# Routed experts: one bf16 one-hot picks bias, position and router weight rows from tables in three parts, the selection is finished on VectorE, and the down projection runs in one piece

## The reference, cut to what matters

```python
logits = hf @ router_w + router_b                    # 32 experts
top_val, top_idx = lax.top_k(logits, 4)
probs = softmax(top_val)                             # comb[token, expert], 0 elsewhere
for e in range(32):
    gu = hf @ w_gate_up[e] + b_gate_up[e]            # 1024 -> 2048
    g, lin = min(gu[:, :1024], 7), clip(gu[:, 1024:], -7, 7)
    act = g * sigmoid(1.702 * g) * (lin + 1)
    out += comb[:, e:e+1] * (act @ w_down[e] + b_down[e])
out = rmsnorm(h + out) * norm_final_g
```

## Time and profile before

| | us |
|---|---|
| median of three runs | 1172.03 |
| the profiled execution: its time | 1168.89 |
| its span, first to last instruction | 1167.1 |
| PE busy | 990.0 (85%) |
| DVE busy | 320.3 (27%) |
| ACT busy | 131.2 (11%) |
| POOL busy | 14.9 (1%) |
| HBM read | 431.69 MB, 371 GB/s over the span |

### The profile page before, as it was taken

How to read it: one execution, slowest core, us unless ns; L and a number is a source line. 1 busy time by engine, 2 the same in 40 slices (tenths; PEclk the granted TensorE clock), 3 DMA queues, 4 the chain that set the end, 5 groups by cost and what they waited for, 6 DMA issues and landing times.

```text
span 1167.1 us, 23860 instructions
## 1 busy us (share of the span) xinstructions
PE 990.0 (85%) x10044; PEld 462.9 (40%) x10045; DVE 320.3 (27%) x949; ACT 131.2 (11%) x292; POOL 14.9 (1%) x26
## 2 busy tenths in 40 slices
PE   8999999999966667689999997699776997977695
PEld 6887886433422222224444332243222342422242
DVE  5999943421211111112212211122111211111112
ACT  2211230500000000000000000000000000000002
POOL 1111000000000000000000000000000000000000
PEclk9999999999998887879999998799878999997898
DMA  9763687695999999997999999999999999999994
GB/s 260 233 169 110 224 331 287 251 424 233 427 427 424 429 424 427 426 427 301 422 411 399 426 426 427 426 425 427 426 425 426 426 426 426 426 426 428 425 426 195
DMA packets 69355, 434.87 MB, mean 373 GB/s; under 512 B 15232, under 2 KB 31552, under 8 KB 36560
## 3 DMA queue, kind: packets, MB, share of 16 engines
q1 hardware_dynamic: 69184, 434.41, 90.9%
q10 hardware_dynamic: 144, 0.09, 0.1%
HBM read 431.69 MB, written 1.05 MB: 371 GB/s over the span
## 4 chain that ended last, share of the span: by engine, by line
PE 45%; DMA 41%; DVE 9%; SPq 3%; issue 2%; ACT 0%; ACTq 0%; DVEq 0%
DMA ring<-in_w_gate_up 24%; PE ps L1478 17%; DMA ring<-in_w_down 13%; PE ps L1491 8%; DMA early<-in_w_gate_up 3%; PE ps L1444 3%; PE ps L1362 2%; PE ps L1413 2%; PE ps L1224 2%; PE ps L1435 2%; PE ps L1467 2%; SPq L369 2%; SPq L366 1%; PE ps L1460 1%; PE ps L1378 1%
## 5 line engine op out<-in xcount | busy, mean ns | idle before, releaser
L1478 PE MATMUL ps<-ring,base 128*32 128x512 f32 x2208 | 294.3, 674 | 115.8 <-DMA ring<-in_w_gate_up 99.4
L1478 PEld LDWEIGHTS ps<-ring,base 128*32 128x32 f32 x2208 | 74.1, 117 | 307.2 <-issue 156.3
L1491 PE MATMUL ps<-ring,base 128*32 128x256 f32 x2944 | 177.5, 381 | 11.5 <-DMA ring<-in_w_down 11.1
L1491 PEld LDWEIGHTS ps<-ring,base 128*32 128x32 f32 x2944 | 89.7, 110 | 101.6 <-issue 33.4
L1131 DVE TENSOR_SCALAR base<-ps 128x256 f32<-128x256 f32 x46 | 19.5, 425 | 379.6 <-PE ps L1478 379.6
L1224 PE MATMUL ps<-ring 128*128 128x256 f32 (+1 forms) x448 | 103.4, 390 | 0.0
L1224 PEld LDWEIGHTS ps<-ring 128*128 128x128 f32 x448 | 84.9, 192 | 15.8 <-issue 1.4
L697 ACT ACTIVATE base<-base 128x256 f32<-128x256 f32 x46 | 19.1, 416 | 628.5 <-DVE base L1131 628.5
L1087 DVE TENSOR_TENSOR base<-ps,base 128x256 f32<-128x256 f32 x47 | 20.0, 425 | 203.3 <-PE ps L1453 203.3
L1478 PE MATMUL ps<-early,base 128*32 128x512 f32 x368 | 52.4, 694 | 16.3 <-DMA early<-in_w_gate_up 16.3
L1478 PE MATMUL ps<-late,base 128*32 128x512 f32 x368 | 50.1, 666 | 13.6 <-DMA late<-in_w_gate_up 13.6
(11 more groups left out here) (323 smaller groups left out, 687.4 us busy)
## 6 DMA issues: line engine op xcount, KB each, us to landing
ring<-in_w_gate_up SPq DMA_DIRECT2D x96, 2048.0 KB, 38.8
ring<-in_w_down SPq DMA_DIRECT2D x63, 2048.0 KB, 40.6
late<-in_w_gate_up SPq DMA_DIRECT2D x16, 2048.0 KB, 40.5
early<-in_w_gate_up SPq DMA_DIRECT2D x16, 2048.0 KB, 39.8
ring<-in_w_in SPq DMA_DIRECT2D x14, 1024.0 KB, 7.8
ring<-in_w_out SPq DMA_DIRECT2D x4, 1024.0 KB, 13.0
ring<-in_w_s_lin SPq DMA_DIRECT2D x2, 1024.0 KB, 6.1
ring<-in_w_s_gate SPq DMA_DIRECT2D x2, 1024.0 KB, 5.4
```

The source lines that it names most:

```text
L1478: ins = nc.tensor.matmul(ps[BS * q:BS * q + BS, 0, :].rearrange("p (a c) -> p a c", a=2), xT[:, k % 2, k // 2, :], row[:, :, QW * q:QW * q ...
L1491: ins = nc.tensor.matmul(ps[BS * q:BS * q + BS, 1, 0:QW], actT[:, n % 2, n // 2, :], row[:, out_cols(q)], start=(n == 0), stop=(n == KT - ...
```

## The change

- **Tables.** b_gate_up is loaded three times, into three groups of 32 partitions, by 12 transfers (4 before), which are issued early, behind the w_in pieces, and not after the layer norm. GpSimd splits them into three bf16 parts that add up to the float32 value: six instructions (three copies, and more, over 4 x 512 elements in each partition), placed between its last tap matrices and the wait for the tap chain. Router weights (three parts) and negated positions go into a second bf16 table, `sel_parts`, built once, ahead of block 0: two extra matmul groups on TensorE and seven instructions on VectorE.
- **Picking.** ebias becomes bf16. bias() is four bf16 matmuls over 96 rows. selection(a, b, at) is four bf16 matmuls of 256 columns that pick a row of sel_parts for all tokens: the position of each token in the expert, and its weight.
- **Finishing.** VectorE copies the gathered rows (which was ScalarE's), copies the picked weights, and forms selT by one scalar_tensor_tensor: position equals the slot's place, times the weight. It no longer builds wsel.
- **Order.** selection of weights, bias and token_columns (which now waits for the copied rows, then does the selection of positions, then the two transposes) all stand between the transposes of the activation and down; down runs in one piece.

```diff
@@ SyncE
             for n in range(4, N_IN - 1):
                 load(n)
+            for g in range(3):
+                for q in range(NQ):
+                    sp.dma_start(bias_in[EXP * g:EXP * g + EXP, q, :].rearrange("e (a c) -> e a c", a=2),
+                                 T["b_gate_up"][0].rearrange("e (a n) -> e a n", a=2)[:, :, QW * q:QW * q + QW]
+                                 ).then_inc(bgu_in, 16)
@@ GpSimd, after its last tap_matrices
+            def split_bias(rows):
+                link(nc.gpsimd.tensor_copy(bias_parts[rows], bias_in[rows]))
+            pool.wait_ge(bgu_in, 16 * 3 * NQ)
+            split_bias(slice(0, 3 * EXP))
+            link(nc.gpsimd.tensor_tensor(bias_in, bias_in, bias_parts, ALU.subtract))
+            split_bias(slice(EXP, 2 * EXP))
+            split_bias(slice(2 * EXP, 3 * EXP))
+            low = slice(2 * EXP, 3 * EXP)
+            link(nc.gpsimd.tensor_tensor(bias_in[low], bias_in[low], bias_parts[low], ALU.subtract))
+            split_bias(low)
+            nc.gpsimd.memset(sel_parts, 0.0).then_inc(bias_split, 1)
             pool.wait_ge(shifts, 16 * MT * SH)
             pool.wait_ge(conv_dve, 1)
@@ ScalarE, in the loop
-                token_rows(i + 1)
-                selection(i + 1)
@@ VectorE, ahead of the loop
+            nc.vector.engine_nop().then_inc(comb_ready, 1)
+            dve.wait_ge(onehot_ready, 1)
+            dve.wait_ge(pos_step, 1)
+            place_of(0)
+            dve.wait_ge(blk_step, 1)
+            next_place(0)
+            dve.wait_ge(pos_tr, 1)
+            nc.vector.tensor_scalar(sel_parts[0:EXP, 0, :], ps[0:EXP, 1, QW:2 * QW], -1.0, None, ALU.mult)
+            dve.wait_ge(selT_ready, 1)
+            weights, rest = selT[0:3 * EXP, :], sel_parts[0:3 * EXP, 1, :]
+            link(nc.vector.tensor_copy(rest, weights))
+            link(TT(comb_rest, weights, rest, ALU.subtract))
+            nc.vector.tensor_copy(rest[EXP:2 * EXP], comb_rest[EXP:2 * EXP])
+            link(nc.vector.tensor_copy(rest[2 * EXP:], comb_rest[2 * EXP:]))
+            link(TT(comb_rest[2 * EXP:], comb_rest[2 * EXP:], rest[2 * EXP:], ALU.subtract))
+            nc.vector.tensor_copy(rest[2 * EXP:], comb_rest[2 * EXP:]).then_inc(sel_rows, 1)
             total = dve.value_load(blk_total[0:1, 0:1], min_val=EXP, max_val=NBLK)
@@ VectorE, one_block
-                for c in range(ST):
-                    ins = nc.vector.tensor_scalar(wsel[:, c, :], slots, cur[:, c:c + 1], cur[:, 2 + c:3 + c],
-                                                  ALU.is_equal, ALU.mult)
+                nc.vector.tensor_copy(place, cur[:, 2:3]).then_inc(place_ready, 1)
...
+                nc.vector.tensor_copy(esel, ebias).then_inc(esel_ready, 1)
                 ebias_for(e)
                 onehot_for().then_inc(onehot_ready, 1)
...
+                dve.wait_ge(gather_mm, i + 2)
+                nc.vector.tensor_copy(xg, ps[:, 2, 0:QW]).then_inc(xg_ready, 1)
+                dve.wait_ge(sel_tr, i + 2)
+                nc.vector.tensor_copy(selT, ps[:, 1, S:2 * S]).then_inc(weights_ready, 1)
                 token_cols(i + 1)
+                dve.wait_ge(weights_ready, i + 1)
+                nc.vector.scalar_tensor_tensor(selT, ps[:, 2, 0:S], place, selT, ALU.is_equal, ALU.mult
+                                               ).then_inc(selT_ready, 1)
@@ TensorE
+            def selection(a, b, at):
+                for q in range(NQ):
+                    ins = nc.tensor.matmul(ps[BS * q:BS * q + BS, b, at:at + S], esel[0:3 * EXP, :],
+                                           sel_parts[0:3 * EXP, a, :], start=True, stop=True, skip_group_check=True,
+                                           tile_position=(0, BS * q))
             def bias():
                 for q in range(NQ):
-                    nc.tensor.matmul(ps[BS * q:BS * q + BS, 0, :], ebias[BS * q:BS * q + EXP, :],
-                                     bias_rows[BS * q:BS * q + EXP, :], start=True, stop=False, skip_group_check=True,
-                                     tile_position=(BS * q, BS * q))
+                    nc.tensor.matmul(ps[BS * q:BS * q + BS, 0, :], ebias[0:3 * EXP, :], bias_parts[:, q, :],
+                                     start=True, stop=False, skip_group_check=True, tile_position=(0, BS * q))
@@ TensorE, middle and outputs_of
                 ins.then_inc(act_tr, 1)
+                selection(1, 1, S).then_inc(sel_tr, 1)
                 bias()
+                token_columns(i + 1)
+                pe.wait_ge(weights_ready, i + 1)
                 pe.wait_ge(actT_ready, i + 1)
                 down(e, odd, 0)
-                token_columns(i + 1)
-                pe.wait_ge(wsel_ready, i + 1)
-                selection(wsel)
                 down(e, odd, 1)
@@ TensorE, block 0
             gate_up(0, 0, 1, 2)
-            pe.wait_ge(blk_step, 1)
-            selection(comb)
+            pe.wait_ge(pos_ready, 1)
+            expert_rows(1, posm, 1).then_inc(pos_tr, 1)
+            pe.wait_ge(comb_ready, 1)
+            expert_rows(3, comb, NQ).then_inc(sel_tr, 1)
             gate_up(0, 0, 2, NPAIR)
+            pe.wait_ge(sel_rows, 1)
```

More of the change, by code:

```diff
@@ L169, in build @@
         hf = [view(rE, 640, D), view(rW, 0, D)]
-        bias_rows = view(rE, 1664, 2 * QW)
+        bias_parts = view(parts, 0, NQ, 2 * QW, rows=3 * EXP, dt=BF16)
+        sel_parts = view(parts, 1024, 2, S, dt=BF16)
+        ebias = view(parts, 1280, BS, dt=BF16)
+        esel = view(parts, 1296, BS, dt=BF16)
+        places = view(parts, 1312, 3, EXP)
+        place = view(parts, 1312 + 3 * EXP, 1)
+        bias_in = view(parts, 1313 + 3 * EXP, NQ, 2 * QW, rows=3 * EXP)
+        comb_rest = view(parts, 1313 + 3 * EXP, S, rows=3 * EXP)
+        comb_all = view(parts, 1313 + 3 * EXP, S)
         squares = view(rW, 0, D)
@@ L676, in _ @@
                     link(nc.scalar.activation(ss[:, 15:16], ss[:, 14:15], ACT.Sqrt))
[L678 to L686 removed]
+            act.wait_ge(gather_mm, 1)
+            nc.scalar.copy(xg, ps[:, 2, 0:QW]).then_inc(xg_ready, 1)
             for c in range(ST):
@@ L690, in _ @@
             link(nc.scalar.activation(ss[:, 15:16], ss[:, 14:15], ACT.Silu))
-            selection(0)
+            act.wait_ge(sel_tr, 1)
+            nc.scalar.copy(selT, ps[:, 3, S:2 * S]).then_inc(selT_ready, 1)
             act.wait_ge(plan, 1)
@@ L1080, in _ @@
             nc.vector.engine_nop().then_inc(blocks_ready, 1)
[L1081 to L1082 removed]
+            nc.vector.engine_nop().then_inc(pos_ready, 1)
+            nc.vector.tensor_copy(places[:, 0:2, :], posm).then_inc(pos_step, 1)
             def token_cols(i):
@@ L1447, in scatter, with token_columns @@
                 return ins
-            def token_columns(i):
+            def token_columns(i, first=False):
                 pe.wait_ge(xg_ready, i + 1)
+                if not first:
+                    selection(0, 2, 0)
                 for j in range(2):
@@ L1549, in _ @@
             gather(1).then_inc(gather_mm, 1)
-            token_columns(0)
+            token_columns(0, first=True)
             pe.wait_ge(blocks_ready, 1)
```

70 lines of the change are left out of this document (32 added, 38 removed).

## The result

The changed kernel takes 1188.54 us (median of 4 runs, 1186.45 to 1190.03), the kernel before beside it 1172.2 us. The ratio is 1.0137, 95% interval 1.0121 to 1.0153: slower by 16.3 us. The forecast was slower by 7.7 us, 1179.7.

The account below looks back on a forecast made before the run. The expert phase was taken as bound by HBM weight transfers, the front by VectorE, which TensorE waits for. Front +14.4 and expert phase -6.7 gave +7.7 on 1172.03, so 1179.7 us, range 1174 to 1185.

Parts of the forecast that it names:

- The front: Before the experts: GpSimd's bias split stops VectorE, so TensorE starts outputs(3) late, with no slack to absorb it: +14.4 us.
- The expert phase: Expert blocks and their start: +2.7 start, -2.8 first three blocks, -4.7 middle, -1.9 end, in sum -6.7 us.
- The split on GpSimd: Bias split stalling VectorE ahead of outputs(3): two tensor_tensors 3.5 us each, four copies 1.85 each, together +14.4.
- The clock: TensorE's clock may fall during its waits ahead of outputs(3): taken as 0, with 2 us as upper bound.
- Block 0's chain: Ahead of block 0: longer VectorE work delays TensorE's activation transposes by 3.1 us, between 1.2 and 3.8.
- A block: Each expert block without waits gets 0.94 us shorter, bounds 0.4 and 1.3.
- The middle: From the wait at 517.14 to the load at 614.58: two shorter blocks and idle queue windows filled, together -4.7 us.
- Behind 614: Nothing until the last piece; behind the wait at 1120.11 two shorter blocks are left: -1.9 us.
- The dearer split: Rival: GpSimd copies at 3.6 us each, or the clock lost in front: 1187 us; chance 0.14.
- The saving doesn't come: Rival: bf16 picks cost as before, or VectorE's longer chain delays down; blocks gain nothing: 1189 us; chance 0.05.
- Hidden: Rival: VectorE's stall from the split is absorbed or far smaller, blocks decide: 1165.3 us, faster; chance 0.13.
- only tensor_tensor: Rival: GpSimd copies do not stop VectorE, only tensor_tensors do: +7.0 - 6.7, 1172.3 us, no change; chance 0.07.

Follow-up runs that it names:

- e1: Kernel before plus the 12 early bias transfers and the GpSimd split (six instructions and memset), result unused: 1187.36 us, ratio 1.0125.
- e2: Changed kernel with the bias split done by VectorE in its wait ahead of the second norm, not by GpSimd: 1171.61 us, ratio 1.0001 to the kernel before.
- e16: Kernel before plus the twelve bias transfers and the split on VectorE, result unused, old float32 bias kept: 1171.42 us, ratio 1.0011.
- e5: e2 with bias() placed behind token_columns instead of ahead of it: 1171.27 us, ratio 0.9990 to the kernel before.
- e17: e12 with the four bias matmuls issued three times over in each bias(), same result: 1170.46 us, ratio 0.9991 to the kernel before.
- e12: Kernel before with only the bf16 bias of the change, split by VectorE ahead of the second norm: 1174.29 us, ratio 1.0027.
- e11: e2 with only the first of three bf16 parts of the router weights, the two lower left out: 1168.08 us, ratio 0.9975 to the kernel before.
- e14: e2 with the router-weight split on GpSimd and bias behind token_columns: 1165.21 us, ratio 0.9959 to the kernel before.
- e10: e2 with the body for even experts ahead of the odd one in TensorE's gate_up and down: 1171.31 us, ratio 0.9995 to the kernel before.

## Why the prediction was right and wrong

The direction and its reason were right, the size was not. The medians tell the two halves of the sum apart. The front, forecast at +14.4, is +15.6 in e1 (14.7 by its ratio), and about 16 between e2 and the changed kernel. The expert phase, forecast at -6.7, is what e2 has: 1.0001, nothing. That is the step that failed, 6.8 of the 8.6 us by which the median was missed. The sum had no term for PE's wait for code, which the shorter bias uncovered (+3.4 in e2), and it took PE's clock as 0 where e2 loses 4.2 us up to its first load. The end gave less than its 1.9, too. VectorE's split may cost e2 a little of this (e16, 1.0011, not clear of 1). That 1188.5 lies inside the stated range is luck.

By its steps, on the pair of profiles, which is 4.8 us dearer than the medians:

- *The split on GpSimd,* +14.4: 14.1. Two errors cancel in part: copies hold 1.57 and not 1.85, tensor_tensors 3.9 and not 3.5. The 32-partition ones cost as much as those of 96. By the Trainium skill (SBUF — State Buffer, Who interferes with whom) GpSimd copies, which read SBUF, stop DVE instructions with two SBUF inputs and a memset does not: the trace agrees, with 1.57 us and with none. The Trainium skill's 4497 ns for a tensor_tensor of 2048 elements (GPSIMD Engine Reference, Elementwise — side-by-side cycle accounting) stand beside 4.49 and 4.44 us here, 4.09 where DVE was quiet.
- *The clock,* taken as 0 with 2 as the bound: the largest miss of this pair. Of the first load's 24.9 us, 14.1 are the stall, 2.5 block 0's chain, 3.7 the gap (4.32 less 0.66), -2.3 three shorter blocks, -0.4 the first bias and -1.15 the difference of the two executions; about 8 are left over, and PE at 1.2 GHz, in the windows above, accounts for them: 2.4 ahead of gate_up(0), 2.1 in it (its first 32 matmuls take 5.96 for 3.84), about 1.6 from the transposes to the end of down(0), 2.5 in the first 32 matmuls behind the gap (6.14 for 3.64). I had looked only at the wait behind outputs(2), where PE had time to spare, and not at 235 to 262, where it had none: gate_up(0) is 2.4 us later than outputs(3)'s delay, and block 0 slower again. e1, with the same stall, has its lower clock in the same places ahead of 255 (0.50 from 235 to 245), and its first load is 18.4 late with outputs(3) 13.0 late. But the 8 us are one execution's, and not the stall's price: between e2 and the changed kernel the ratios leave about 2 us above the 14.1, in e1 0.6 to 1.5. That the stall sets off the lower clock at 235 isn't shown: e5, without it, has 0.54 from 225 to 235, and e17 1.00. What does stays open. The profile of the kernel before, with 1.00 there, is one of its fastest executions (1168.89; all its runs 1168.72 to 1175.47), so a typical one may lose some of this too.
- *No term for code:* +3.7 us ahead of block 2, and what its clock behind costs. The prediction counted the shorter bias as pure gain and did not ask what it had covered. e12, where it is the one change to the loop, has the gap, and e17, with the cover back, has not.
- *Block 0's chain,* +3.1: +2.0 from the copy to the transposes, and 0.45 for the positions' rows. e11, without five of the six instructions, starts its first down 1.9 us sooner than e2; the rest of its 2.8 at the first load is the clock behind the gap, less 0.3 of a longer gap.
- *A block,* -0.94: before, loads that follow one another are 15.80 and 15.26 us apart, after 14.91 and 14.65, so 0.75 in the mean. The bf16 prices were right: 0.54 for the three groups, forecast 0.51. What was missing is the issue gap of 0.32 us at the branch ahead of down in even blocks, which the old bias hid: odd blocks are 0.9 shorter, even ones 0.6 (14.90 for 15.52). The bf16 bias in front of the branch, in e14, doesn't hide it.
- *The middle,* -4.7: from 303.15 to 635.66 the lag falls by 3.8; in e2, from 6.9 to 2.2, by 4.6.
- *Behind 614,* -1.9: nothing came, +0.1. The lag grows by 1.0 to the wait at 1142.17, the last two blocks give 1.6, and the last scatter ran at the lower clock, 1.89 us for 1.15. In e2, too, the whole stretch gave 1.2.

So the pair's 21.1 less the forecast 7.7, 13.4, are: clock about 8.4, code 3.7, the end 2, the middle 0.9, less 1.2 by which this execution was ahead in front and less 0.4 for small terms. The dearer split of the rivals named 1187 and the clock, but mostly for copies at 3.6 us, which was wrong. *The saving doesn't come* named 1189, which is nearly what was measured, and its outcome is what e2 shows; but its cause was wrong, since the blocks are 0.6 to 0.9 us shorter. *Hidden* and *only tensor_tensor* are ruled out by the DVE rows.

## What to carry to other kernels

An idle GpSimd is no free engine while VectorE is what others wait for: look at VectorE's row beside each GpSimd row before you place work there, and put it where VectorE stands. Before you make an instruction on the path cheaper, ask what waits behind it that it covers, a semaphore or the loading of a loop's code on its first passes; e17 got 0.36% back by computing a bias three times. A delay of an engine that never waits again is paid in full, and more than in full where its clock falls.

## What the runs showed of the hardware that was not expected

- TensorE's first passes over a loop of some 16 KB pieces of code can cost it 2 to 4.4 us. It restarts 4.2 to 4.3 us behind the piece in 16 of the 17 kernels with a bf16 bias, and 0.4 us more of matmuls ahead of a wait and a branch took the gap from 3.34 to 0.67 us (e17). Where the order of the bodies was turned, the gap was in two places (e10).
- A branch into the body that lies second cost TensorE 0.3 us (even blocks in e2, odd ones in e10). A float32 bias of 1.06 us ahead of it hid all but 0.03, four bf16 matmuls of 0.4 us hid almost nothing.
- The lower clock behind such a gap doesn't follow its length alone: from 265 to 275 us it is 0.83 in e5 (2.96 us) and 1.00 in e12 (3.34 us).
- A GpSimd cast of 2048 float32 elements to bf16 takes 2.3 us for 32 partitions beside DVE, 1.9 alone. VectorE's own takes 1.22 (e2).
